# A fused transformer-and-MoE step: experts in straight code, a seventh weight slot in the place of the residual, and the residual kept in the output tensors

## What is computed

```python
def _hier_moe(x, router_group, router_expert, w_gate, w_up, w_down):
    ...
    expert_id = g_idx * EXPERTS_PER_GROUP + e_idx        # 4 groups of 8, the top 2 of one group
    gates = jnp.sum(jax.nn.one_hot(expert_id, N_EXPERTS, dtype=jnp.float32) * weights[..., None], axis=1)
    hid = jax.nn.silu(jnp.einsum('td,edf->tef', t, w_gate)) * jnp.einsum('td,edf->tef', t, w_up)
    y = jnp.einsum('tef,efd->td', hid * gates[:, :, None], w_down)

def _layer(...):
    ...
    x = x + gate1 * _rms_norm(mix, g_post_mix)
    h2 = _rms_norm(x, g_pre_ffn) * (1 + scale2) + shift2
    f = _hier_moe(h2, ...)
    x = x + gate2 * _rms_norm(f, g_post_ffn)
```

## Time and profile before

| | us |
|---|---|
| median of 3 runs | 674.0 (673.79 to 677.46) |
| the profiled execution, its own time | 672.75 |
| its span, first to last instruction | 671.0 |
| PE busy | 548.3 (82%) |
| DVE, ACT, POOL busy | 192.8, 151.3, 173.5 |
| DRAM read and written | 163.23 MB and 14.58 MB |

### The profile page before, as it was taken

How to read it: one execution, slowest core, us unless ns; L and a number is a source line. 1 busy time by engine, 2 the same in 40 slices (tenths; PEclk the granted TensorE clock), 3 DMA queues, 4 the chain that set the end, 5 groups by cost and what they waited for, 6 DMA issues and landing times.

```text
span 671.0 us, 9726 instructions
## 1 busy us (share of the span) xinstructions
PE 548.3 (82%) x3055; PEld 301.5 (45%) x3056; DVE 192.8 (29%) x575; ACT 151.3 (23%) x375; POOL 173.5 (26%) x240
## 2 busy tenths in 40 slices
PE   0479999999987789999997789899998878788700
PEld 0235654444354455455554445455554444444300
DVE  1150312001367763244467102011111111111037
ACT  2630102002126663232221011111111111111142
POOL 1000000002513332143335423334332222221212
PEclk9999999999998999999998899999998898899955
DMA  8999108054199300620044959999999999999183
GB/s 254 401 404 397 65 1 312 1 193 183 37 312 409 124 2 1 219 95 31 33 166 143 409 220 407 395 392 408 405 395 401 402 404 393 406 403 395 47 327 157
DMA packets 53192, 170.23 MB, mean 254 GB/s; under 512 B 7660, under 2 KB 8340, under 8 KB 52256
## 3 DMA queue, kind: packets, MB, share of 16 engines
q1 hardware_dynamic: 46112, 155.45, 60.1%
q0 software_dynamic: 6752, 14.13, 5.9%
q10 hardware_dynamic: 288, 0.13, 0.1%
HBM read 163.23 MB, written 14.58 MB: 265 GB/s over the span
## 4 chain that ended last, share of the span: by engine, by line
PE 54%; DMA 26%; DVE 8%; ACT 4%; SPq 3%; issue 3%; PEld 1%; PEldq 0%; POOL 0%; ACTq 0%; POOLq 0%; DVEq 0%
DMA ring<-in_w_down_dram 12%; PE ps L722 10%; PE ps L619 10%; PE ps L869 8%; PE ps L600 5%; PE ps L520 5%; DMA w<-in_w_down_dram 5%; DMA ring<-in_w_mod_dram 4%; PE ps L877 4%; PE ps L601 3%; PE ps L699 2%; PE ps L539 2%; DMA ring<-in_w_up_dram 2%; ACT probs L1495 2%; DVE probs L1130 1%
## 5 line engine op out<-in xcount | busy, mean ns | idle before, releaser
L869 PE MATMUL ps<-ring,xt 128*64 128x256 f32 x768 | 97.3, 410 | 19.9 <-DMA ring<-in_w_up_dram 12.3
L869 PEld LDWEIGHTS ps<-ring,xt 128*64 128x64 f32 x768 | 64.7, 148 | 58.6 <-issue 36.6
L619 PE MATMUL ps<-ring,h_t 128*128 128x512 f32 x160 | 69.5, 594 | 0.0
L1365 DVE TENSOR_TENSOR hid<-act_g,ps 128x128 f32<-128x128 f32 x32 | 9.2, 287 | 185.7 <-ACT act_g L1572 185.7
L722 PE MATMUL ps<-ring,mix_t 128*128 128x512 f32 x120 | 53.6, 596 | 0.0
L1699 POOL DMA_INDIRECT expert_results<-y_sb,idx_out x32 | 32.7, 1023 | 58.3 <-ACT y_sb L1586 55.4
L619 PEld LDWEIGHTS ps<-ring,h_t 128*128 128x128 f32 x160 | 30.1, 190 | 37.6 <-issue 37.6
L869 PE MATMUL ps<-w,xt 128*64 128x256 f32 x352 | 40.4, 382 | 6.0 <-DMA w<-in_w_up_dram 4.1
L877 PE MATMUL ps<-ring,hid_t 128*64 128x512 f32 x176 | 42.6, 605 | 3.2 <-ACT hid_t L1582 2.6
L600 PE MATMUL ps<-ring,h_t 128*128 128x512 f32 x80 | 42.0, 607 | 2.7 <-DVE h_t L1022 2.7
L1628 POOL TENSOR_TENSOR gm_stats<-gm_stats,half_pow 128x8 f32<-128x8 f32 x5 | 9.7, 1939 | 129.5 <-DVE gm_stats L1088 129.5
(11 more groups left out here) (238 smaller groups left out, 725.5 us busy)
## 6 DMA issues: line engine op xcount, KB each, us to landing
ring<-in_w_mod_dram SPq DMA_DIRECT2D x8, 3072.0 KB, 20.2
ring<-in_w_gate_dram SPq DMA_DIRECT2D x22, 1024.0 KB, 9.3
ring<-in_w_up_dram SPq DMA_DIRECT2D x22, 1024.0 KB, 13.7
ring<-in_w_down_dram SPq DMA_DIRECT2D x22, 1024.0 KB, 16.0
w<-in_w_gate_dram SPq DMA_DIRECT2D x10, 1024.0 KB, 8.6
w<-in_w_up_dram SPq DMA_DIRECT2D x10, 1024.0 KB, 13.6
w<-in_w_down_dram SPq DMA_DIRECT2D x5, 1024.0 KB
w_6d<-in_w_down_dram SPq DMA_DIRECT2D x5, 1024.0 KB, 16.2
```

Of the source, the lines that this page charges most:

```text
L619: last = pe.matmul(ps[:, 4 + u % 4, :], h_t[:, k, i * P:(i + 1) * P], w[:, k, :], start=(k == 0), stop=(k == KC - 1))
L869: last = pe.matmul(bank[fh * SLOT:(fh + 1) * SLOT, 0:FE].rearrange("p (a f) -> p a f", a=2), x_t[:, k % 4, (k // 4) * SLOT:(k // 4 + 1) * ...
```

## The change

- All engines run the 32 experts in straight code: there is no loop over them, and row and semaphore numbers are constants. LATE = 26 keeps the last six in the late order. In that order PE now does the products of e+1 before it turns `xg` of e+2, and DVE, ACT and POOL follow.
- WS = 7. The seventh place is `w_7` (gate and up, 2 MB) on the first four tiles of `res`, and `w_7d` (down, 1 MB) beside `w_6d`. Weight semaphores repeat with period LS = 4.
- The residual of the tiles 0 to 3 (KEPT = 4) is stored in the output tensors by DMAs from ACT, as each tile is finished. Tile 4 stays in `res`.
- The loads of the experts 3 to 6 come in pieces, each as soon as its place is free: gate and up of expert 6, expert 3, down of 5, down and up of 4, gate of 4, gate and up of 5, down of 6. The store of the last tile of `h2` moves from SP to ACT.
- The second gate goes to `gate_f`, in the place of slot 4, when expert 25 is done. The residual of tile 3 is read back there too (`res_back`).
- At the end the tiles 0, 1 and 2 (ADDED = 3) are not added on DVE: their gated rows go to `y_out`, and POOL adds them into the outputs by accumulating DMAs. The tiles 3 and 4 are added on DVE as before.
- Some semaphores are merged (`s_rows` into `s_const`, `s_gmn` into `s_ws`, `s_xre` into `s_wr`), `keep_warm` reads other tiles, and `shift_b` lies elsewhere.

```diff
-WS = 6
+WS = 7
...
-LS = 3
-LOOPED = (EXPERTS - 2 - WS) // WS
+LS = 4
+LATE = EXPERTS - 6
+KEPT = TILES - 1
+ADDED = 3
+GATE_SLOT = 25
...
+        w_7 = sb("w_7", [P, 2 * KC * FE], F32, res_at)
+        w_7d = sb("w_7d", [P, KC * FE], F32, gates_at + 8 * KB)
+        gate_f = sb("gate_f", [P, 2, D], F32, b0)
+        res_back = sb("res_back", [P, D], F32, b0 + 8 * KB)
...
+            sp.wait_ge(t2_tr, 2 * KEPT)
+            sp.wait_ge(h2_mul, 2 * KEPT)
+            sp.wait_ge(sq3, 2 * KEPT)
+            sp.wait_ge(res_out, 16 * KEPT)
+            load_half(6, 0)
+            load_half(6, 1)
             s, v = USED[ITEMS[N_FIRST - 1]]
             sp.wait_ge(s, v)
...
-            def reload(q, c):
-                e = q * WS + c
+            for e in range(WS, EXPERTS):
                 sp.wait_ge(y_mm, e - WS + 1)
                 sp.wait_ge(expert_done, e - WS + 1)
-
-                sp.sem_inc(seen, 1)
-                load_landed(*nth(q, c, -2))
-                load_expert(q, c)
...
+                load_landed(e - 2)
+                load_expert(e)
+
+            sp.wait_ge(y_mm, GATE_SLOT + 1)
+            sp.wait_ge(expert_done, GATE_SLOT + 1)
+            sp.dma_start(gate_f[:], gates_dram[1:2].broadcast_to((P, 2, D))).then_inc(gate_in, 16)
+            sp.dma_start(res_back[:], out_rows(KEPT - 1)).then_inc(gate_in, 16)
...
+                if late and e + 1 < EXPERTS:
+                    products(e + 1)
                 if late and e + 2 < EXPERTS:
-                    next_x(*nth(q, c, 2))
-                if late and e + 1 < EXPERTS:
-                    products(*nth(q, c, 1))
+                    next_x(e + 2)
...
-                    link(dve.scalar_tensor_tensor(y_sum[:, i - 1], y_sum[:, i - 1], stats[:, 7, i - 1:i],
-                                                  gate_bc[:, 1, cond_of(i - 1), :], ALU.mult, ALU.mult))
-                    dve.tensor_tensor(y_out[:, i - 1], res[:, i - 1], y_sum[:, i - 1], ALU.add).then_inc(f_out, 1)
+                    to = y_out if i <= ADDED else y_sum
+                    gated_ = dve.scalar_tensor_tensor(to[:, i - 1], y_sum[:, i - 1], stats[:, 7, i - 1:i],
+                                                      gate_f[:, cond_of(i - 1), :], ALU.mult, ALU.mult)
+                    if i <= ADDED:
+                        gated_.then_inc(f_out, 1)
+                    else:
+                        link(gated_)
+                        dve.tensor_tensor(y_out[:, i - 1], res[:, KEPT] if i - 1 == KEPT else res_back[:],
+                                          y_sum[:, i - 1], ALU.add).then_inc(f_out, 1)
...
+                if i < KEPT:
+                    act.dma_start(out_rows(i), res[:, i]).then_inc(res_out, 16)
+                else:
+                    act.wait_ge(h2_done, 2 * TILES)
+                    act.dma_start(h2_dram[i * P:(i + 1) * P, :], h2[:, i % 2]).then_inc(h2_out[i % 2], 16)
...
+            pool.wait_ge(res_out, 16 * KEPT)
+            for i in range(TILES + 1):
+                if i < TILES:
+                    pool.wait_ge(f_ms, i + 1)
+                    rsqrt(stats[:, 7, i:i + 1], stats[:, 6, i:i + 1], 1, f_rs)
+                if 1 <= i <= ADDED:
+                    pool.wait_ge(f_out, i)
+                    pool.dma_start(out_rows(i - 1), y_out[:, i - 1], accum_op=ALU.add).then_inc(f_add, 16)
```

More of the change, by code:

```diff
@@ L449, in _ @@
                 sp.wait_ge(s, v)
[L450 removed]
+                load_expert(j)
             sp.wait_ge(s_pre2, 2)
@@ L1380, in expert @@
                     dve.tensor_tensor(hid_x[:, :], act_x[:, :], ps[:, 2 + c % 2, P:2 * P], ALU.mult).then_inc(e_hid, 1)
+                if late and e + 1 < EXPERTS:
+                    hidden(e + 1)
                 if late and e + 2 < EXPERTS:
-                    copy_x(*nth(q, c, 2))
-                if late and e + 1 < EXPERTS:
-                    hidden(*nth(q, c, 1))
+                    copy_x(e + 2)
             extra_counts()
-            copy_x(0, 0)
+            copy_x(0)
             extra_tiles()
-            copy_x(0, 1)
-            hidden(0, 0)
+            copy_x(1)
+            hidden(0)
             extra_rows()
-            all_experts(dve, expert)
+            for e in range(EXPERTS):
+                expert(e)
             def weighted(i):
@@ L1597, in expert @@
                 if late and e + 1 < EXPERTS:
-                    silu(*nth(q, c, 1))
-            silu(0, 0)
+                    silu(e + 1)
+            silu(0)
             act.wait_ge(rows_made, ALL_ROWS)
-            all_experts(act, expert)
+            for e in range(EXPERTS):
+                expert(e)
             def first_result(i):
@@ L1741, in _ @@
             gather_extra(0)
-            def expert(q, c):
-                e = q * WS + c
-                late = is_late(e)
-                if not late:
-                    gather_ahead(*nth(q, c, 2))
-                scatter(q, c)
+            for e in range(EXPERTS):
+                if e < LATE:
+                    gather_ahead(e + 2)
+                scatter(e)
                 extras(e)
-                if late and e + 2 + XS < EXPERTS:
-                    gather_ahead(*nth(q, c, 2))
-            all_experts(pool, expert)
+                if e >= LATE:
+                    gather_ahead(e + 2)
             n_extra = pool.value_load(extra_at[0:1, EXPERTS:EXPERTS + 1], min_val=0, max_val=MAX_EXTRA)
```

277 lines of the change are left out of this document (128 added, 149 removed).

## The result

The changed kernel takes **667.3 us** (663.97 to 668.42, 4 runs) against 674.5 us (673.79 to 677.46, 4 runs): a ratio of **0.989**, 95% interval 0.986 to 0.992. The forecast was 666.2, in a range of 660 to 672. The profiled execution took 668.42 us with a span of 666.5, against 672.75 and 671.0 before.

A forecast was written before the change was run, and what follows sets the result against it. The prediction took the expert stage to be bound by the weights' arrival, for lack of a place. Its terms, -8.7 + 3.0 + 0.5 - 2.6 = -7.8, took the 674.0 us median to 666.2 us, range 660 to 672.

The forecast's parts named there:

- (a): Expert loads: a seventh place filled early moves every later load one step ahead; -8.7 us, bounds -7.5 and -9.5.
- (d): End: three of five adds leave DVE for accumulating DMAs that land unnoticed; -2.6 us, bounds -1 and -3.7.
- (c): Expert code: removing loops gains nothing, fetching 0.3 to 0.4 MB more instructions costs; +0.5 us, bounds -1 and +2.
- The weights decide: Products of expert 30: up weights land at about 603.3 us, after PE's own chain could arrive at 601.1.
- (b): Start of the experts: early loads delay the last `h2` store and first gathers; +3 us, bounds 0 and +6.
- The rule that would have made (b) +1: DMA engines alternate between queues with work, so the `h2` store needs about twice its own 1.3 us beside the weights.
- The sign that the forecast names for (d): At the end, DVE's last add comes about 27 us after the last scatter in place of 28.7.
- 1 (the start gives it back): Start: store and gathers each wait in the queue and PE cools down, +6 us there; 670.4 us; chance 0.15.
- 2 (all hidden): Whole kernel: early loads delay the first gathers by 0, the other terms come out better; 661.0 us; chance 0.17.
- 3 (slow accumulates): End: accumulating DMAs run one after another, three times t each; 683.1 us at t = 10 us; chance 0.08.
- 4 (late instructions): Last ten experts: instruction fetches queue behind weights, 4 us each; two of them give 674.2 us; chance 0.07.
- 5: Early loads: expert 6's halves load late because SP waits, so the seventh place gains nothing; 674.9 us; chance 0.03.

The follow-up runs named there:

- straight code alone: The kernel before with its loops over the experts written out, still six places and the old end: 675.4 us, ratio 1.0016.
- six places: The changed kernel with the seventh place left empty, expert 6 loaded only when expert 0 is done: 671.15 us, ratio 0.996.
- turn-first kernel: The changed kernel with the old late order, `xg` turned ahead of the next expert's products: 667.24 us, ratio 0.9898.
- 3 MB behind the gathers: The changed kernel with down of 4 and 5 and up of 4 loaded after the first three gathers: 663.55 us (0.9841), again 665.25 us (0.9872).

## Why the prediction was right

The forecast's four terms and the pieces of the traces both add up to -7.8, and that they agree so closely is in part luck. The loads gave 1.2 us less than (a), and the end 0.3 us less than (d). Three things make up for it: 0.5 us less between load 31 and the last scatter, which no term had; a first reload that came 2.5 us later and not 3; and the 0.5 us of (c), which has no piece of its own.

**(a) The seventh place, forecast -8.7.** The mechanism is as forecast: the window at 386 to 393 us is mostly idle, seven experts' weights are there in time, and a step is gone from the row of loads. The size is a little smaller: against the straight code alone the loads take 8.2 us less, against six places 7.6. The last step of before, 8.67 us, was taken for the gain; in the second trace of before it is 8.16. Net of what filling the place costs at the start, it is worth the 4.4 to 5.1 us of the six-place kernel. "The weights decide" held: the products of expert 30 waited 0.36 us for up weights (0.97 and 0.95 in the other two traces), and counted from `st_bc` they started at 329.6, where the forecast's own numbers (612.38 - 8.7 + 3.0 + 0.5, less 277.16) give 330.0. PE's waits for up weights at the products of the experts 28 to 30 add up to 0.4, 1.9 and 3.7 us in the three traces, around the 2.4 us that the forecast left between PE and the weights. With the turn first the same working gives PE 568.2 + 35.5 = 603.7 beside 603.5 for the weights, a tie, and the turn-first kernel did reach the same time.

**(b) The first gathers, forecast +3.** The first gather left 3.7 us later than before and the products started 3.1 us later in the mean (+2.3 to +3.9 between single traces); the first reload is 2.5 us later. The step went in the way described, and larger: the store took 7.7 us, not 6.5, the gather behind it 3.8 and not 4. After the longer pause the products of expert 0 took 4.7 to 5.4 us in place of 3.67, so that at the extra tile's turn the delay was 4.0 us, though its gather was 0.5 us faster. Of these, 1.5 us came back before the first reload, and not by the queue: SP issued it 1.1 us behind the extra tile's last product, 2.1 us before (1.3 in the straight code alone, so this belongs to (c)), and the extra tile's turn and products were 0.5 us shorter. Against the straight code alone, (b) is 3.7 us; both are within the bounds 0 to 6.

The rule that would have made (b) +1 held for one part of the store's time and left out the other. SP's queue (q1) and ACT's (q10), first from 358.3 us, when the store is issued, to 361.9, and then from 363 to 365 us:

```profile
q1 hardware_dynamic: 340, 1.32, 101.8%
```

```profile
q1 hardware_dynamic: 118, 0.42, 51.7%
q10 hardware_dynamic: 106, 0.40, 49.6%
```

In the Trainium skill ("DMA: Bandwidth & Descriptors", Queues, rings and completion order) each engine takes turns between its queues. The trace agrees with that once the store's packets move: the two queues have the engines half and half. But the first packet moves only 3.85 us after the issue (3.5 to 3.9 us in all eight traces with full engines, 0.84 us in the three where 3 MB stood behind the gathers), and in that time weights pass alone, 1.3 to 1.4 MB. The working by the rule had no such wait. What causes it is open: the store was moved from SP's queue to ACT's with the change, and it was not run on SP's.

**(c) Straight code, forecast +0.5.** Alone it cost 1.1 us (ratio 1.0016, its interval includes 1), 0.6 between the traces. Its two sides are larger than the sum shows: -1.2 us at the start, 0.8 of it between the extra tile's last product and the first reload, and +0.7 in the loads.

**(d) The end, forecast -2.6.** Scatter to last add -3.2, and +0.9 from there on: -2.3. In the forecast the accumulates landed unnoticed. The last of them, issued at 657.0, did land before the end, but it was under way until about 663, and the two last stores, issued at 659.7 and 662.1, took 4.0 to 4.4 us, not 2.6 to 3.0. The working had put 0.5 us on POOL's queue, which the trace doesn't show (3.2 of the 3.7 us came through on DVE), and nothing on the stores; the two errors nearly cancel, which is luck. The sign that the forecast names for (d), a last add 27 us behind the last scatter, doesn't follow from its own sum, which has that add start at 664.7 - 1.2 - 637.5 = 26.0 us behind it; it was 25.4.

**The rivals.** 1 (the start gives it back): half true. Its parts are in the traces (the store's wait, and products of 4.7 to 5.4 us after the pause), but they came to 2.5 to 3.7 us, not to 6. 2 (all hidden): the kernel with 3 MB behind the gathers is this case for (b), and came to 663.6 and 665.3 us, not 661.0. 3 (slow accumulates): they took twice a plain store's time, 5.8 us, above the 4.4 us from which the working let them pass the end, below 8.1; they come 2.5 us apart and overlap, so the line 3t was too pessimistic. 4 (late instructions): no wait of that size stands in the trace, and straight code alone cost 0.6 to 1.1 us. 5: no, the seventh place fills from 341 us on.

## What to carry over

Where a stage waits for weights, one more slot brings at most one load's time (7.6 us here), less what filling it costs others (4.4 to 5.1 us were left). A small store and a dependent gather in the same window pay for the full engines: price these first, and start bulk loads behind the last short transfer that someone waits for. Here that brought 4 us at the start and likely 2.3 us in all. Read how two queues share from a stretch in which both have work; over a longer one the small transfer's share only says how small it is. Where two limits lie within 1 us of each other (here the weights and PE's late order), undoing one of them alone shows nothing.

## What the runs showed of the hardware

- A store of 512 KB on ACT's queue took 7.2 to 8.2 us when 2 to 3 MB of weights were still queued on SP's, and 3.0 us when they were not. Its first packet moved 3.5 to 3.9 us after the issue, with 2 MB as with 3 MB, and 0.84 us where the engines were free. Once it moved, the two queues shared evenly (51.7% and 49.6% of the engines' time from 363 to 365 us).
- After a pause of PE of 2.4 to 4.3 us the products of expert 0 took 4.2 to 5.7 us, at a granted clock of 0.73 in the changed kernel's first trace; in the kernel before, where PE had been busy up to them, they took 3.67 us at 1.00.
- An accumulating DMA of 512 KB into DRAM landed in 5.5 to 5.8 us, a plain one from the same place in 2.9 to 3.0. Issuing it took POOL 0.86 to 1.00 us in place of 0.57 to 0.64. Plain stores issued 2.6 and 5.1 us behind the last of three took 4.0 to 4.4 us.
- The code ahead of the experts ended anywhere between 277.2 and 281.2 us, both in traces of one and the same kernel. That spread of 4 us is half of what the change brings, so single spans of two kernels can't be compared without taking it out.
